# A three-layer block on one core: another order at the launch, and two weight parts split later in the second block

## The chip, the cores and the metric

The kernel runs on one core of one Trainium2 chip. The metric is the device time of one execution in microseconds (us), the median over several runs. In the rows, PE is TensorE's matmul side and PEld its weight load, DVE is VectorE, ACT ScalarE, POOL GpSimd, SP SyncE; SPq, ACTq and POOLq are DMA issues on the queues of these engines.

## The reference

One sequence of 256 tokens of width 1024 in fp32. Twice (`l` = 0, 1) a block of four mixers, cross attention and an MLP; then a second block with its own mixers and a mixture of experts. Cut to what the change touches:

```
h = rms_norm(x, ln_mix_pre[l]);  z = h @ w_in[l]        # l = 0 is the launch
s = q @ k.T * scale + bias_f[t5_bucket(t - s)]          # rel_bias, the same for both l

# second block
log_a = 8 * sigmoid(gate_r) * log_sigmoid(lam);  a = exp(log_a)
u = sqrt(-expm1(2 * log_a)) * (sigmoid(gate_i) * xr)
h = scan over time of h = a * h + u                     # the recurrence
y_c = conformer_conv(xc)                                # 31 taps, layer norm, silu, 256x256
y = concat(rms_norm(y_a), rms_norm(h * gelu(xg)), rms_norm(y_c))
x = x + y @ w_out                                       # then router and 32 experts
```

## The kernel before, in words

Each engine has a program of its own, written out by hand (`tensor`, `scalar`, `vector`, `pool`, `sync`), and nothing reorders it: an instruction behind a waiting one waits too. `P["name"]`, `A[...]`, `V[...]` are counts of what PE, ACT and DVE have finished.

**Units.** All large weights come as units of up to 1 MB through a ring of four slots, loaded by SP in order (`load`). A unit is used in two parts: ACT copies its rounded high part (`upper`, L1306, `hl<-ring`), DVE subtracts to get the low part (`lower_part`, L1953), and PE multiplies three times (`mm3`). `unit()` on ACT and DVE splits up to `LOOK` = 2 units ahead of the one that PE is about to use. SP loads a unit into a slot when the low part of the unit that had it is made. Four units of the second block, the convolution's taps, are not split (`whole`): PE reads them raw, and their slots come free only when PE is done with them:

```
if had is not None and (whole(had) or P.way == "few" and had >= n_ring):
    sp.wait_ge(s_pe, P["unit", had])
elif had is not None:
    sp.wait_ge(s_dve, V["lo", had])
```

**Launch.** ACT's queue loads constants `cst` (with the identity for transposes), parameters `par`, `x` (to `resid`) and `CO` (to `arena`: mask and one-hot rows for the bias). All engines wait for all four. PE makes `rowb`, the bias by distance; ACT copies it out; POOL writes it to memory and reads it back with every row shifted by one (`hank`, `arena<-scratch`); PE turns these rows (`C("rev")`, four matmuls `psum<-arena,cst` 128x384 called "bias"), DVE adds the mask, POOL stores the result (`bias_d<-arena`, semaphore `s_bias`). Beside it run the first norm (ACT Square and Sqrt, DVE scale by the gain `gn`), PE's transposes, and the cuts of the turned x into high and low parts (`norm_cut`, into `ht`). ACT and DVE wait for `s_bias` and only then split units 0, 1, 2; PE then runs the projections `kcks`, `q`, `kw` (units 0, 1, 2: 48, 48 and 24 matmuls) and `vg` (unit 3).

**Second block.** On PE: projections, scores (`z`) of head groups 0 to 2, `zx`, sums (`cum`) 0 and 1, `xg`, `taps(0)`, the gates `wa` and `wx`, sums 2, `weighted` 0 and 1, `taps(1)`, scores 3, `weighted` 2, `taps(2)`, sums 3, `taps(3)`, a group norm, `cmean`, `weighted` 3, `cvar` and on to the output projection `tok_out(axv, "bout")` with the four units of the output weights, here w0 to w3. w0 goes into the slot of `taps(0)`, w1 into that of `taps(1)`. The recurrence's lane on ACT and DVE: tanh of the gates, `t3` = tanh(log a), `uvar`, its root `ustd`, two scans, the gelu product, `gnsq`; head group 3 goes between (`logits`, `keeps`, `log_keep`, `log_weight`).

Of the kernel before, what the change touches and what calls it, by code (L numbers as in the profile page):

```python
# [21 lines left out]
LOOK = 2  # L22
# [240 lines left out]
def build(nc, W, CW, CS, CO, PR, PR2, GB, x_in, mem_in, out, scratch, bias_d, gate_d):  # L263
    ctx = ExitStack()
    with ctx:
# [96 lines left out]
        m0 = Place()  # L362
# [205 lines left out]
        def tensor(pe, branch):  # L568
# [3 lines left out]
            def bank(*name, keep=False):  # L572

                b, before = turn.keep(name) if keep else turn.take(name)
                if before in freed:
                    of, n = freed[before]
                    pe.wait_ge(of.sem, n)
                banks[name] = b
                return b

            def mm(o, pairs, start=True, stop=True, skip=False):
                n = len(pairs)
                for i, (a, b) in enumerate(pairs):
                    ins = pe.matmul(o, a, b, start and i == 0, stop and i == n - 1, skip)
                return ins
# [89 lines left out]
            pe.wait_ge(s_const, 16)  # L675
            pe.wait_ge(s_par, 16)
            pe.wait_ge(s_x, 16)
            pe.wait_ge(s_once, 16)
            b = bank("rowb")
            mm(psum[0:4, b, :], [(R("rel")[0:32, :], m0.onehot[0:32, :])]).then_inc(s_pe, P("rowb"))  # L680
            for l in range(2):
                L = layers[l]
                norm(L.nmix.xn, "mix", l)
                if l == 0:
                    pe.wait_ge(s_hank, 32)
                    for h in range(4):
                        b = bank("bias", h)
                        mm(psum[:, b, 0:384], [(C("rev"), m0.hank[:, h, :])]).then_inc(s_pe, P("bias", h))
# [3 lines left out]

                pe.wait_ge(s_dve, V["mix", l])
                proj(hTv, "kcks", l)
                proj(hTv, "q", l)
# [587 lines left out]
        def scalar(ac, branch):  # L1283
# [65 lines left out]
            def inverse_root(o, eps, scale, *name):  # L1349
# [4 lines left out]
                act(o, o, ACT.Exp, *name, scale=-0.5)  # L1354

            ac.dma_start(cst[:, :], CS).then_inc(s_const, 16)
            ac.dma_start(par[:, :], PR).then_inc(s_par, 16)
            ac.dma_start(Xv, x_in.rearrange("b (t p) d -> p (b t) d", t=2)).then_inc(s_x, 16)
            ac.dma_start(arena[:, 0:896], CO[:, 0:896]).then_inc(s_once, 16)
            ac.wait_ge(s_const, 16)  # L1360
            ac.wait_ge(s_par, 16)
            ac.wait_ge(s_x, 16)
            ac.wait_ge(s_once, 16)
            ac.wait_ge(s_pe, P["rowb"])
            copy(m0.rowb[0:4, :], psum[0:4, banks["rowb",], :], "rowb")
            gone("rowb")
            for l in range(2):
                L = layers[l]
                if l == 0:
                    for t in range(2):  # L1370
                        norm(Xv, L.nmix, t, "mix", l)
                    for t in range(2):
                        norm_cut(hTv, t, "mix", l)
                if l == 0:
                    ac.wait_ge(s_bias, 16)
# [370 lines left out]
            gone("xg")  # L1746
            for _ in range(4):
                unit()
            for nm, dst, o in (("wa", t1, 0), ("wx", t2, 2)):
# [12 lines left out]
            ac.wait_ge(s_dve, V["uvar"])  # L1762
            act(t1, t1, ACT.Sqrt, "ustd")
            ac.wait_ge(s_dve, V["gelu"])
            act(t3, t3, ACT.Tanh, "gelu", scale=math.sqrt(2.0 / math.pi))
            weights(3)
            ac.wait_ge(s_pe, P["cu"])
# [132 lines left out]
        def vector(ve, branch):  # L1900
# [97 lines left out]

            ve.wait_ge(s_const, 16)
            ve.wait_ge(s_par, 16)  # L2000
            ve.wait_ge(s_x, 16)
            ve.wait_ge(s_once, 16)
            for l in range(2):
                L = layers[l]
                if l == 0:
                    for t in range(2):
                        norm(Xv, L.nmix, t, "mix", l)
                    for t in range(2):
                        norm_cut(hTv, t, "mix", l)
                    for h in range(4):  # L2010
                        ve.wait_ge(s_pe, P["bias", h])
                        tt(m0.bm[:, h, :], psum[:, banks["bias", h], 0:384], m0.causal, ADD, "bias")
                        gone("bias", h)
                    ve.wait_ge(s_bias, 16)
# [463 lines left out]
            unit()  # L2478
            for _ in range(4):
                unit()  # L2480
            ve.wait_ge(s_act, A["lam"])
# [14 lines left out]
            ve.wait_ge(s_act, A["t3"])  # L2496
            ts(t1, t3, -1.0, None, ADD, None)
            rec(t1, t1)
            stt(t1, t3, 2.0, t1, MUL, MUL, "uvar")
            tt(t3, b2.xg, b2.xg, MUL)  # L2500
# [10 lines left out]
            tt(t3, b2.yc[1], b2.yc[1], MUL, "gnsq", 1)  # L2511
            log_weight(3)
            ve.wait_ge(s_act, A["ya", 2])
            tt(b2.zq[:, 0:3, :], b2.yc[0][:, 0:3, :], b2.yc[0][:, 0:3, :], MUL)
# [175 lines left out]
        def pool(gp, branch):  # L2690
# [22 lines left out]

            gp.wait_ge(s_const, 16)
            gp.wait_ge(s_par, 16)
            gp.wait_ge(s_x, 16)
            gp.wait_ge(s_once, 16)
            gain("mix0")
# [291 lines left out]
```

## Time and profile before

| | us |
|---|---|
| median of 3 runs (lowest, highest) | 2109.21 (2103.8, 2111.39) |
| the profiled execution, its own time | 2104.69 |
| its span | 2102.9 |
| PE busy in the span | 1915.1 (91%) |
| DVE busy | 1426.7 (68%) |
| ACT busy | 1168.5 (56%) |

1.79 us lie outside the span. Mean granted clock of TensorE 0.961. The page's line of 40 slices shows PE at 7 to 9 tenths everywhere but in the first slice (4), with three slices of 7 in a row at 28 to 30 (1419 to 1577 us: the end of the second block's mixers, and the router), and the DMA engines at 9 tenths and some 375 GB/s only in the experts' stage, slices 31 to 39.

### The profile page before, as it was taken

Reading aid. Unit: us, or ns where it says so; the run is one execution under the profiler, and the core shown is the slowest. Engines: PE = TensorE matmul, PEld = TensorE weight load, DVE = VectorE, ACT = ScalarE, POOL = GpSimd, SP = SyncE. Lnnn points to the kernel's source line nnn. Section 1 sums busy time; section 2 is a strip of 40 time slices with the busy share of each in tenths; the row PEclk is TensorE's granted clock in tenths of the full one; section 3 lists DMA queues with packets and bytes.
Section 4 is the critical chain, followed back from the end, with each engine's and each line's share of the span. In section 5 each row is a group of like instructions: output and inputs, shape, how many; then the busy total and the mean of one; then the engine's idle time right before and its main releaser. Section 6 shows DMA issues by size and latency. Waiting matters only on the chain.

```text
span 2102.9 us, 30304 instructions
## 1 busy us (share of the span) xinstructions
PE 1915.1 (91%) x12946; PEld 1747.3 (83%) x12946; DVE 1426.7 (68%) x1425; ACT 1168.5 (56%) x1310; POOL 76.5 (4%) x94
## 2 busy tenths in 40 slices
PE   4999997988999889997997999897779999999997
PEld 3989997987998889997997999796668888888885
DVE  3686547545555677637645555755679999999995
ACT  2644344544444554333644444454368888888884
POOL 0000013000000000013000000000000000000000
PEclk9999998998999999999998999998879999999998
DMA  7333374524554333356542555332259999999993
GB/s 265 127 141 136 119 266 162 200 101 142 193 189 159 156 141 131 127 178 243 186 159 105 190 195 181 134 121 86 94 224 374 375 375 380 377 379 374 375 391 135
DMA packets 64524, 440.87 MB, mean 210 GB/s; under 512 B 7372, under 2 KB 7372, under 8 KB 14592
## 3 DMA queue, kind: packets, MB, share of 16 engines
q1 hardware_dynamic: 55296, 399.63, 50.6%
q0 software_dynamic: 8096, 35.30, 4.5%
q10 hardware_dynamic: 992, 3.93, 0.5%
q8 instruction: 104, 1.70, 0.3%
q14 instruction: 36, 0.29, 0.0%
HBM read 428.61 MB, written 10.23 MB: 209 GB/s over the span
## 4 chain that ended last, share of the span: by engine, by line
PE 65%; DVE 22%; ACT 8%; issue 2%; POOL 1%; DMA 1%; DVEq 0%; ACTq 0%; POOLq 0%
PE psum L188 64%; DVE ring_low L202 6%; ACT hl L198 3%; DVE arena L212 3%; DVE ht L202 2%; DVE rounded L202 2%; DVE rounded L212 2%; DVE arena L202 2%; ACT arena L198 1%; PE psum L192 1%; POOL arena L202 1%; DVE hl L202 1%; ACT rounded L198 1%; DVE arena L225 1%; DVE resid L202 1%
## 5 line engine op out<-in xcount | busy, mean ns | idle before, releaser
L202 DVE TENSOR_TENSOR hl<-ring,hl 128x2048 fp32r<-128x2048 f32 (+1 forms) x190 | 433.9, 2286 | 350.7 <-ACT hl L198 350.3
L188 PE MATMUL psum<-ht,hl 128*128 128x256 f32 x4992 | 630.2, 288 | 15.4 <-DVE hl L202 9.7
L188 PEld LDWEIGHTS psum<-ht,hl 128*128 128x128 f32 x4992 | 616.2, 195 | 25.1 <-DVE hl L202 10.3
L198 ACT ACTIVATE hl<-ring 128x2048 fp32r<-128x2048 f32 (+1 forms) x286 | 536.3, 1896 | 150.7 <-PE psum L188 122.9
L188 PE MATMUL psum<-hl,ax 128*128 128x512 f32 (+1 forms) x1608 | 351.9, 355 | 6.4 <-DVE ax L202 5.0
L198 ACT ACTIVATE arena<-psum 128x512 f32<-128x512 f32 (+5 forms) x232 | 121.0, 522 | 418.5 <-PE psum L188 405.5
L188 PEld LDWEIGHTS psum<-hl,ax 128*128 128x128 f32 x1608 | 264.8, 192 | 47.3 <-DVE ax L202 5.3
L202 DVE TENSOR_TENSOR ring_low<-ring,hl 128x2048 fp32r<-128x2048 f32 x96 | 215.3, 2285 | 19.3 <-ACT hl L198 19.1
L188 PE MATMUL psum<-arena 128*128 128x128 f32 (+6 forms) x1520 | 190.8, 291 | 30.1 <-ACT arena L198 23.5
L188 PEld LDWEIGHTS psum<-arena 128*128 128x128 f32 (+2 forms) x1520 | 174.7, 179 | 41.6 <-ACT arena L198 25.2
L188 PE MATMUL psum<-hl,ht 128*128 128x256 f32 (+1 forms) x1056 | 132.2, 287 | 26.8 <-DVE ht L212 24.0
L188 PEld LDWEIGHTS psum<-hl,ht 128*128 128x128 f32 x1056 | 129.9, 196 | 29.0 <-DVE ht L212 24.4
L188 PE MATMUL psum<-rounded 128*128 128x512 f32 (+2 forms) x640 | 137.5, 346 | 8.7 <-DVE rounded L202 3.1
L188 PEld LDWEIGHTS psum<-rounded 128*128 128x128 f32 x640 | 104.0, 197 | 25.9 <-issue 7.1
L202 DVE TENSOR_TENSOR arena<-arena 128x512 f32<-128x512 f32 (+8 forms) x133 | 87.0, 654 | 46.3 <-ACT arena L198 40.2
L202 DVE TENSOR_TENSOR rounded<-arena,hl 128x2048 fp32r<-128x2048 f32 x48 | 107.7, 2286 | 0.2
L202 DVE TENSOR_TENSOR ht<-ht_raw,hl 128x2048 fp32r<-128x2048 f32 x46 | 103.2, 2285 | 5.4 <-ACT hl L198 5.4
L188 PE MATMUL psum<-hl,hx 128*128 128x512 f32 x256 | 101.4, 396 | 1.3 <-ACT rounded L198 1.3
L188 PE MATMUL psum<-hl,rounded 128*128 128x512 f32 x256 | 101.6, 397 | 0.0
L188 PE MATMUL psum<-ax,hl 128*128 128x256 f32 x768 | 94.1, 284 | 0.0
L188 PEld LDWEIGHTS psum<-ax,hl 128*128 128x128 f32 x768 | 92.7, 192 | 1.0 <-issue 1.0
L198 ACT ACTIVATE hl<-arena 128x2048 fp32r<-128x2048 f32 x48 | 89.2, 1913 | 0.0
(121 smaller groups left out, 1897.7 us busy)
## 6 DMA issues: line engine op xcount, KB each, us to landing
ring<-W SPq DMA_DIRECT2D x284, 1024.0 KB, 5.1
arena<-W SPq DMA_DIRECT2D x48, 1024.0 KB, 7.5
ht_raw<-W SPq DMA_DIRECT2D x46, 1024.0 KB, 7.8
gate_d<-arena POOLq DMA_DIRECT2D x32, 256.0 KB, 3.8
arena<-gate_d POOLq DMA_DIRECT2D x8, 1024.0 KB, 8.0
gn<-GB POOLq DMA_DIRECT2D x10, 512.0 KB, 4.1
arena<-GB POOLq DMA_DIRECT2D x6, 512.0 KB, 4.9
ring<-W SPq DMA_DIRECT2D x4, 512.0 KB, 4.5
```

The lines of the kernel that those rows point to most:

```text
L188: return Nothing() if self.e is None else self.e.matmul(o, a, b, start=start, stop=stop, skip_group_check=skip_group_check)
L192: return Nothing() if self.e is None else self.e.transpose(o, a, ident)
L198: return self.e.activation(o, a, f, bias=bias, scale=scale)
L202: return Nothing() if self.e is None else self.e.tensor_tensor(o, a, b, op)
L212: return Nothing() if self.e is None else self.e.scalar_tensor_tensor(out=o, in0=a, scalar=s, in1=b, op0=op0, op1=op1)
L225: return Nothing() if self.e is None else self.e.reciprocal(o, a)
```

## The change

At the launch, `x` is the first load of ACT's queue, ahead of the constants. ACT, DVE and POOL no longer wait for everything: ACT and DVE run both norms of x on `s_x` alone, then split unit 0, and wait for constants, parameters and `CO` behind it; ACT's copy of `rowb` stands there too; POOL's load of the gain waits for nothing. Units 1 and 2 are split behind the cuts, ahead of the wait for `s_bias`. PE runs `kcks` ahead of the turned rows ("bias"). SP's waits are as they were.

In the second block the four `unit()` calls of the taps, which split w0 and w1, move down on ACT (from behind the copy of `xg` to behind the gelu's tanh) and on DVE (from ahead of the lambda chain to behind `log_weight(3)`). And `uvar` is worked out in another way: a*a + 1 times tanh(log a), with the sign taken in the root's scale, in place of 2 t3 / (t3 - 1): a subtraction, a reciprocal and a product of 128x512 become two products.

```diff
@@ tensor @@
-            b = bank("rowb")
-            mm(psum[0:4, b, :], [(R("rel")[0:32, :], m0.onehot[0:32, :])]).then_inc(s_pe, P("rowb"))
             for l in range(2):
                 L = layers[l]
+                if l == 0:
+                    pe.wait_ge(s_par, 16)
+                    pe.wait_ge(s_once, 16)
+                    b = bank("rowb")
+                    mm(psum[0:4, b, :], [(R("rel")[0:32, :], m0.onehot[0:32, :])]).then_inc(s_pe, P("rowb"))
                 norm(L.nmix.xn, "mix", l)
                 if l == 0:
+                    pe.wait_ge(s_dve, V["mix", l])
+                    proj(hTv, "kcks", l)
                     pe.wait_ge(s_hank, 32)
@@ scalar @@
+            ac.dma_start(Xv, x_in.rearrange("b (t p) d -> p (b t) d", t=2)).then_inc(s_x, 16)
             ac.dma_start(cst[:, :], CS).then_inc(s_const, 16)
             ac.dma_start(par[:, :], PR).then_inc(s_par, 16)
-            ac.dma_start(Xv, x_in.rearrange("b (t p) d -> p (b t) d", t=2)).then_inc(s_x, 16)
...
                         norm(Xv, L.nmix, t, "mix", l)
+                    upper()
+                    ac.wait_ge(s_const, 16)
+                    ac.wait_ge(s_par, 16)
+                    ac.wait_ge(s_once, 16)
+                    ac.wait_ge(s_pe, P["rowb"])
+                    copy(m0.rowb[0:4, :], psum[0:4, banks["rowb",], :], "rowb")
+                    gone("rowb")
                     for t in range(2):
                         norm_cut(hTv, t, "mix", l)
-                if l == 0:
+                    for _ in range(LOOK):
+                        upper()
                     ac.wait_ge(s_bias, 16)
...
             gone("xg")
-            for _ in range(4):
-                unit()
             for nm, dst, o in (("wa", t1, 0), ("wx", t2, 2)):
...
-            act(t1, t1, ACT.Sqrt, "ustd")
+            act(t1, t1, ACT.Sqrt, "ustd", scale=-1.0)
             ac.wait_ge(s_dve, V["gelu"])
             act(t3, t3, ACT.Tanh, "gelu", scale=math.sqrt(2.0 / math.pi))
+            for _ in range(4):
+                unit()
             weights(3)
@@ vector @@
                         norm(Xv, L.nmix, t, "mix", l)
+                    lower_part()
+                    ve.wait_ge(s_const, 16)
+                    ve.wait_ge(s_par, 16)
+                    ve.wait_ge(s_once, 16)
                     for t in range(2):
                         norm_cut(hTv, t, "mix", l)
+                    for _ in range(LOOK):
+                        lower_part()
...
             unit()
-            for _ in range(4):
-                unit()
             ve.wait_ge(s_act, A["lam"])
...
-            ts(t1, t3, -1.0, None, ADD, None)
-            rec(t1, t1)
-            stt(t1, t3, 2.0, t1, MUL, MUL, "uvar")
+            tt(t1, aL, aL, MUL)
+            stt(t1, t1, 1.0, t3, ADD, MUL, "uvar")
...
             log_weight(3)
+            for _ in range(4):
+                unit()
             ve.wait_ge(s_act, A["ya", 2])
@@ pool @@
-            gp.wait_ge(s_const, 16)
-            gp.wait_ge(s_par, 16)
-            gp.wait_ge(s_x, 16)
-            gp.wait_ge(s_once, 16)
             gain("mix0")
```

How the instructions stand on the engines, at two places.

ACT at the program's start, before, from the first table load on (`hl<-ring` are the units 0, 1 and 2; `tensor_done` and so on are the counts of the other engines, `once_in` is `s_once`, `bias_in` is `s_bias`):

```order
L198 ACT_TABLE_LOAD [waits once_in,x_in,tensor_done,par_in]
L198 ACTIVATE arena<-psum 4x512 [waits const_in]
L199 ACTIVATE arena<-resid 128x512 x2
L198 ACT_TABLE_LOAD [waits scalar_done]
L198 ACTIVATE arena<-arena 128x1 [waits vector_done]
L199 ACTIVATE arena<-resid 128x512 x2
L198 ACTIVATE arena<-arena 128x1 [waits scalar_done,vector_done]
L198 ACTIVATE ht<-psum 128x4x128 [waits tensor_done] x4
L198 ACTIVATE hl<-ring 128x2048 [waits tensor_done,weights_in0,vector_done,bias_in]
L198 ACTIVATE hl<-ring 128x2048 [waits weights_in1]
L198 ACTIVATE hl<-ring 128x1024 [waits weights_in2]
```

The same place in the changed kernel:

```order
L199 ACT_TABLE_LOAD
L199 ACTIVATE arena<-resid 128x512 [waits x_in]
L199 ACTIVATE arena<-resid 128x512
L198 ACT_TABLE_LOAD [waits scalar_done]
L198 ACTIVATE arena<-arena 128x1 [waits vector_done]
L199 ACTIVATE arena<-resid 128x512 x2
L198 ACTIVATE arena<-arena 128x1 [waits scalar_done,vector_done]
L198 ACTIVATE hl<-ring 128x2048 [waits weights_in0]
L198 ACTIVATE arena<-psum 4x512 [waits tensor_done,once_in,scalar_done,par_in,const_in]
L198 ACTIVATE ht<-psum 128x4x128 [waits tensor_done] x4
L198 ACTIVATE hl<-ring 128x2048 [waits weights_in1]
L198 ACTIVATE hl<-ring 128x1024 [waits weights_in2]
```

The first table load now waits for nothing, the copy of `rowb` (4x512) went from ahead of the norm to behind it and unit 0, and no unit stands behind `bias_in` any more.

DVE in the second block, the difference of the two kernels from the lambda chain to the squares of the attention's groups (`hl<-ring` x2 are w0 and w1, the `arena<-arena,psum` x2 with the next row are `log_weight(3)`):

```order
-L208 TENSOR_SCALAR arena<-arena 128x512
-L225 RECIPROCAL arena<-arena 128x512
+L202 TENSOR_TENSOR arena<-arena 128x512
 L212 SCALAR_TENSOR_TENSOR arena<-arena 128x512
 L202 TENSOR_TENSOR arena<-arena 128x512
```

```order
 L202 TENSOR_TENSOR arena<-arena,psum 128x384 x2
 L208 TENSOR_SCALAR arena<-arena 128x768
+L202 TENSOR_TENSOR hl<-ring,hl 128x2048 x2
 L202 TENSOR_TENSOR arena<-arena 128x768
 L212 SCALAR_TENSOR_TENSOR arena<-psum,arena 128x512
```

The two low parts left the place ahead of the lambda chain and stand between `log_weight(3)` and the squares that precede the product of `cmean` (the last row); in `uvar` the reciprocal is gone.

## Rows read from the trace of the kernel before

**Rows 1.** Stretch: length, busy us of PE, PEld, DVE, ACT, POOL, clock, DMA, GB/s.

```profile
1600.00:1650.00 50.00, 48.75 (x253) 40.30 (x251) 47.84 (x35) 43.90 (x38) 0.00 (x0) 1.00 0.96 378
```

**Rows 2.** DMA of 0 to 40 us: one GB/s figure per us, and issues to landing.

```profile
GB/s 0 115 107 369 410 427 459 351 418 422 409 412 126 74 442 426 389 422 412 403 21 0 69 290 373 82 324 168 4 0 0 0 233 418 135 0 80 319 432 438
cst<-CS ACTq DMA_DIRECT2D x1, 1027.0 KB, 7.9
bias_d<-arena POOLq DMA_DIRECT2D x1, 768.0 KB, 3.5
arena<-CO ACTq DMA_DIRECT2D x1, 448.0 KB, 10.8
```

**Rows 3.** Timeline of the launch: start, us, instructions merged, [idle before <-releaser].

```profile
13.10 1.86 PE L188 MATMUL psum<-arena,par 32*4 32x512 f32 x2 [13.10 <-DMA arena<-CO]
16.36 0.59 ACT L198 ACTIVATE arena<-psum 4x512 f32<-4x512 f32 x1
16.85 0.61 ACT L199 ACTIVATE arena<-resid 128x512 f32<-128x512 f32 x1
...
18.25 1.28 ACT L198 ACT_TABLE_LOAD   x1
...
22.41 0.29 ACT L198 ACTIVATE arena<-arena 128x1 f32<-128x1 f32 x1 [1.36 <-DVE arena L209]
...
23.75 1.97 PE L192 MATMUL psum<-cst,arena 128*128 128x128 f32 x8 [0.27 <-DVE arena L212]
...
25.86 4.31 PE L188 MATMUL psum<-arena,cst 128*128 128x384 f32 x7
...
34.96 4.66 ACT L198 ACTIVATE hl<-ring 128x2048 fp32r<-128x2048 f32 x3 [8.61 <-DMA bias_d<-arena]
...
37.87 5.56 DVE L202 TENSOR_TENSOR hl<-ring,hl 128x2048 fp32r<-128x2048 f32 x3
40.24 15.90 PE L188 MATMUL psum<-ht,hl 128*128 128x256 f32 x120 [9.75 <-DVE hl L202]
47.53 0.80 ACT L198 ACTIVATE arena<-psum 128x256 f32<-128x256 f32 x2 [7.91 <-PE psum L188]
...
55.98 5.48 PE L188 MATMUL psum<-hl,ht 128*128 128x140 f32 x48
```

**Rows 4.** Stretches, same columns: PE's restart at 40.2 us, and 1443 to 1453 us.

```profile
40.20:43.20 3.00, 2.96 (x14) 2.99 (x15) 3.00 (x2) 0.00 (x0) 0.00 (x0) 0.51 0.91 336
1443.00:1453.00 10.00, 5.88 (x22) 4.72 (x23) 8.85 (x21) 5.44 (x9) 0.00 (x0) 0.51 0.01 2
```

**Rows 5.** Timeline of the second block, PE.

```profile
1428.11 7.18 PE L188 MATMUL psum<-arena,ring 128*128 128x256 f32 x32
1443.04 1.65 PE L188 MATMUL psum<-arena 128*128 128x256 f32 x4 [7.10 <-ACT arena L198]
1448.77 2.00 PE L188 MATMUL psum<-arena 128*64 128x128 f32 x12 [4.08 <-ACT arena L198]
...
1460.88 6.21 PE L188 MATMUL psum<-arena,ring 128*128 128x256 f32 x28
```

**Rows 6.** The same stretch, ACT.

```profile
1440.00 1.91 ACT L198 ACTIVATE hl<-ring 128x2048 fp32r<-128x2048 f32 x1 [10.16 <-DMA ring<-W]
...
1451.35 1.72 ACT L198 ACTIVATE arena<-arena 128x768 f32<-128x768 f32 x2 [0.39 <-DVE arena L212]
...
1457.17 0.63 ACT L198 ACTIVATE arena<-arena 128x512 f32<-128x512 f32 x1
```

**Rows 7.** The same stretch, DVE.

```profile
1451.89 3.35 DVE L225 RECIPROCAL arena<-arena 128x512 f32<-128x512 f32 x1
...
1458.00 1.76 DVE L212 SCALAR_TENSOR_TENSOR arena<-arena 128x768 f32<-128x768 f32 x2
...
1465.41 0.96 DVE L202 TENSOR_TENSOR arena<-arena 128x768 f32<-128x768 f32 x1
1469.40 0.69 DVE L212 SCALAR_TENSOR_TENSOR arena<-psum,arena 128x512 f32<-128x512 f32 x1 [3.03 <-PE psum L188]
```

More of the change, by code:

```diff
@@ L675, in tensor @@
             pe.wait_ge(s_const, 16)
-            pe.wait_ge(s_par, 16)
-            pe.wait_ge(s_x, 16)
-            pe.wait_ge(s_once, 16)
-            b = bank("rowb")
-            mm(psum[0:4, b, :], [(R("rel")[0:32, :], m0.onehot[0:32, :])]).then_inc(s_pe, P("rowb"))
             for l in range(2):
                 L = layers[l]
+                if l == 0:
[3 more added lines that the diff above has]
+                    mm(psum[0:4, b, :], [(R("rel")[0:32, :], m0.onehot[0:32, :])]).then_inc(s_pe, P("rowb"))
                 norm(L.nmix.xn, "mix", l)
                 if l == 0:
+                    pe.wait_ge(s_dve, V["mix", l])
+                    proj(hTv, "kcks", l)
                     pe.wait_ge(s_hank, 32)
@@ L690, in tensor @@
                 fill = filler(l)
-                pe.wait_ge(s_dve, V["mix", l])
-                proj(hTv, "kcks", l)
+                if l:
+                    pe.wait_ge(s_dve, V["mix", l])
+                    proj(hTv, "kcks", l)
                 proj(hTv, "q", l)
@@ L1354, in inverse_root @@
                 act(o, o, ACT.Exp, *name, scale=-0.5)
+            ac.dma_start(Xv, x_in.rearrange("b (t p) d -> p (b t) d", t=2)).then_inc(s_x, 16)
             ac.dma_start(cst[:, :], CS).then_inc(s_const, 16)
             ac.dma_start(par[:, :], PR).then_inc(s_par, 16)
-            ac.dma_start(Xv, x_in.rearrange("b (t p) d -> p (b t) d", t=2)).then_inc(s_x, 16)
             ac.dma_start(arena[:, 0:896], CO[:, 0:896]).then_inc(s_once, 16)
-            ac.wait_ge(s_const, 16)
-            ac.wait_ge(s_par, 16)
             ac.wait_ge(s_x, 16)
[L1363 to L1366, printed above, removed]
             for l in range(2):
@@ L1997, in wide @@
                 return ap.broadcast_to([128, ap.shape[1], n])
-            ve.wait_ge(s_const, 16)
-            ve.wait_ge(s_par, 16)
             ve.wait_ge(s_x, 16)
-            ve.wait_ge(s_once, 16)
             for l in range(2):
```

## The prediction

> **What bounds the kernel now.** I read the stages first, by stretches. In the experts' stage nothing of this change takes part: in 50 us PE is busy 48.75 and DVE 47.84, the granted clock is 1.00 and DMA runs at 378 GB/s [rows 1]. It will come as it is, earlier or later. So the question is only when PE gets its work in the two edited places, and there I read the timeline and the chain of waits.
>
> *Launch.* The first matmul starts at 13.10, released by the load of `CO` [rows 3]. DMA runs at some 410 GB/s from 4 to 11 us [rows 2], so the early loads are bound by bandwidth and not by their issue. Then one lane runs: `rowb` on PE, ACT's copy at 16.36, two small transfers by POOL, the turned rows on PE at 25.86, masks, `bias_d`, and at 34.96 ACT, released by it, begins unit 0 [rows 3]. PE's row at 40.24 says idle for 9.75 us before, waiting for DVE's low part. x, unit 0 and the turned x were all there long before 34.96: the projections wait for splits that stand behind a semaphore they don't need.
>
> *Second block.* PE finishes `taps(1)` at 1435.3 [rows 5]. Half of scores 3 follows, and then PE stands 7.10 us for ACT. ACT's row at 1440.00 tells why: it waited 10.16 us for a DMA, which is w1 [rows 6]. w1's slot is free only when `taps(1)` is done. Behind this wait stand the tanh of the gates, which give PE the bank for the other half. Then come 4.08 us more for `weighted` 2. The granted clock from 1443 to 1453 is 0.51, the low level (1.2 GHz), after this idling [rows 4].
>
> **The change, launch.** Its loads: `cst`, first in the queue, took 7.9 us [rows 2], so x in its place (1024 KB against 1027) lands at 0.74 + 7.9 = 8.6. The gain, 512 KB, now goes at once too: 1.3 us at 410 GB/s. I take x at 9.3 (8.6 to 9.9) and `CO` 1.3 later than now, at 14.3.
>
> By x: from the first Square at 16.85 to the second root's end at 22.70 are 5.85 us, of which some 0.7 were a wait for the gain, gone now; ACT's first table load waits for nothing and is hidden. So 9.3 + 5.2 = 14.5, unit 0's high part 1.9 (a share of 4.66 for three), low part 2.2 (of 5.56 for three [rows 3]), four cuts of 0.69 (a 128x512 DVE operation, [rows 7]): 21.4. By `CO`: 14.4, `rowb` 1.9, sixteen transposes in two lots of 1.97 [rows 3], one cut on ACT and DVE, 1.3: 21.5. The two paths are equal; I take 21.5 for `kcks` against 40.24.
>
> `kcks` ran 7.25 us (40.24 until ACT's copy at 47.53, where 72 matmuls then took 8.65), because PE restarts at the low level: 0.51 in its first 3 us [rows 3, 4]. It will again: PE stands 1.5 us before, and the rates of the first 30 us are low-level ones though the record has no mark there (the turned rows take 4.31 for 7 records of 384 columns, 1.6 ns a column; taps at a clock of 1.00 take 0.87 [rows 3, 5]). `kcks` ends at 28.8.
>
> The bias lane: ACT reaches the copy of `rowb` at 16.4, PE has it at 16.3; it began at 16.36 before. So the turned rows land as before, at 25.9, and 3 us of `kcks` cover them. That is the slack for SP's loads: units 4 and 5 now follow the low parts at 18.7 and 24, beside POOL's two transfers, and 1 MB is 2.5 us of bandwidth. From the first turned matmul to `s_bias` it was 34.96 - 25.86 = 9.1. PE is warm now, which takes 2.2 off (8 records of 384 columns at 0.87 in place of 1.6): 6.9, so `s_bias` comes at 35.7, later than now by 0.7.
>
> Who waits for `s_bias`: ACT and DVE, for unit 3 only, since 0 to 2 are split. DVE's memsets took it from 34.96 to 37.9, then the low part of unit 3, 1120 columns, 1.3 at the pace of [rows 3]: 40.0. PE: 28.8 + 2.7 of turned rows + 8.65 for `q` and `kw` = 40.2. Again equal. `vg` starts at 40.3 against 55.98, **15.7 us** earlier, and from there on everything stands in its old order. If `s_bias` is late beyond 0.2 us each us counts in full; if x or `CO` is late, too. Ends: 11 (x 1.5 late, and 3 for transfers beside each other), 17.5 (x at 8.6 and `kcks` warm after its first 1.5 us).
>
> By the Trainium skill ("ScalarE: Activation LUTs", What ACT_TABLE_LOAD costs) a switch is a load of about 1.28 us and a drain of about 1.38. The row at 18.25 shows 1.28, and the span of 5.85 contains all that followed, so no drain is added here. By the page's figure the path by x would be 1.4 longer and this term 14.3.
>
> **The change, second block.** The wait for w1 leaves ACT's way. The gates' banks are free at about 1427, so PE goes through 1435.94 (1443.04 less 7.10) without a stop. From 1443.04 to the end of `taps(3)` at 1467.1 are 24.05 us; without 4.08 of waiting, and with the 5.9 us of matmuls in the slow stretch [rows 4] at twice the clock (2.9 less), 17.1 remain: `taps(3)` ends at 1453.0, **14.1** earlier.
>
> Can DVE's lane follow? Scores 3 are in by 1437.7 (1435.94 + 0.8 of matmul + 0.9). From `keeps(3)` at 1451.35 to the end of `ustd` at 1457.80 it was 6.45 [rows 6]: 1444.2. Removed on DVE are the reciprocal, 3.35, and a subtraction of 0.4, added is a product of 0.7 [rows 7]: with it DVE's own work ends at 1441.1, hidden behind ACT's `keeps(3)`; with the old form it would end at 1444.2 and delay `log_keep(3)` by about 2.5. From the scaled input of the scan (1459.0) to the squares (1465.41) are 6.4: 1450.6. Here the two low parts come in, 2 x 2.3 = 4.6: 1455.2, squares 0.96: 1456.2, and the product of `cmean` starts then, against 1469.40: **13.1** earlier. PE has `cmean` ready at 1455.3, so the moved low parts cost 0.9 of the 14.1. ACT's share of w0 and w1 (3.8) lies from 1446.4 to 1450.2, before the weights of group 3 are asked for at 1450.6: hidden, with 0.4 to spare. w1's load landed at 1440: covered. Behind that stand the same instructions; w2 and w3 load behind `taps(2)` and `taps(3)`, 14 earlier. Ends: 9 (the lane pays all 4.6) and 14.2 (PE's own).
>
> **Sum.** 15.7 + 13.1 = 28.8 off the profiled execution's 2104.69: 2075.9; off the median 2109.21: 2080.4. The profiled run lies near the lowest of the three; I say 2078. Ends: 20 to 31.7 off, 2073 to 2089.
>
> **Rivals.** (a) The bias lane sets the launch. `hank` and `bias_d` now share the DMA engines with units 4 to 6. For: bandwidth is full at 410 GB/s when several loads run; `CO`, 448 KB behind others, took 10.8, `bias_d` 3.5 [rows 2]. If both of POOL's late transfers take 10.8, that is 7.3 on `bias_d` and 3 or more past the slack on the rows: the launch gives 5, the sum 18: 2089. Against: from 22 to 35 us the figures of [rows 2] lie mostly below 330 and often at 0. Chance 0.12.
> (b) The second block gives half. The chain there is carried by DVE, whose unit parts were free in the wait, and some step that I count as hidden isn't: 6.5 in place of 13.1, 2085. For: DVE's slack in my sum is negative already. Chance 0.12.
> (c) No change: PE's work between the edited places is re-timed, and later waits (POOL's gate transfers, loads) take back over 20 us, 2100. Against: nothing in the program is tied to the time since its start. 0.04.
> (d) Slower: a busier PE is granted less. If the clock in the experts' stage, about 540 us long with PE busy 97%, fell below 1.00, each hundredth would cost 5 us; from 0.05 on it eats the gain, from 0.08 on the time ends above 2115. Against: the clock was 1.00 there at PE's densest [rows 1]. 0.02.
> My forecast, both terms within their ends: 0.70.
>
> **The numbers.** Forecast, (a) and (b) lie between 2066 (lowest run 2103.8, both upper ends, some noise) and 2092; I give 2066 to 2094. Such a kernel is told from no change at about 0.5%, 10.5 us: faster is below 2098.7. Faster 0.70 + 0.12 + 0.12 = 0.94; same 0.04; slower 0.02.
>
> **What the profile will show.** Right: the first Square near 9.5 us; `kcks` near 21.5; turned rows behind it near 29; `vg` near 40.3 with no PE idle between `kcks` and `vg` above 1 us. In the second block no PE gap between `taps(0)` and `taps(3)`, clock 1.00, the two low parts on DVE right behind `log_weight(3)`, and about 13 us less from `xg` to `cmean`'s product. Wrong: PE idle ahead of `q` or `vg` waiting for `bias_d` or DVE (a); PE idle ahead of sums 3 or more than 1 us ahead of `cvar` (b).

## The result, and the profile after

The changed kernel takes 2084.89 us, median of 4 runs (2082.65 to 2085.21), against 2108.58 of 4 runs of the kernel before (2103.8 to 2111.39): a ratio of 0.9888, with an interval of 0.9868 to 0.9907. It is faster. The forecast was 2078 with a range of 2066 to 2094. The profiled execution took 2085.21, its span is 19.6 shorter than that of before, and 28.8 had been forecast.

The page, its first and third line:

```profile
span 2083.3 us, 30300 instructions
...
PE 1918.9 (92%) x12946; PEld 1752.3 (84%) x12946; DVE 1423.3 (68%) x1424; ACT 1167.9 (56%) x1310; POOL 76.5 (4%) x94
```

PE is busy 3.8 us longer than before with the same work, while the span is shorter: a first sign that it ran more of it at a lower clock.

The launch, timeline of all engines (start, duration, then as in [rows 3]):

```profile
10.17 0.63 ACT L199 ACTIVATE arena<-resid 128x512 f32<-128x512 f32 x1 [6.07 <-DMA resid<-x]
...
11.59 1.28 ACT L198 ACT_TABLE_LOAD   x1
12.88 0.29 ACT L198 ACTIVATE arena<-arena 128x1 f32<-128x1 f32 x1
...
14.90 1.86 PE L188 MATMUL psum<-arena,par 32*4 32x512 f32 x2 [14.90 <-DMA arena<-CO]
...
22.07 6.02 PE L188 MATMUL psum<-ht,hl 128*128 128x256 f32 x48 [1.71 <-DVE ht L202]
27.92 2.74 PE L188 MATMUL psum<-arena,cst 128*128 128x384 f32 x8
...
31.61 0.54 POOL L231 DMA_DIRECT2D bias_d<-arena  x1 [9.08 <-DVE arena L202]
...
36.71 0.80 ACT L198 ACTIVATE arena<-psum 128x256 f32<-128x256 f32 x2 [12.96 <-DMA bias_d<-arena]
...
39.61 1.26 DVE L202 TENSOR_TENSOR hl<-ring,hl 128x1120 fp32r<-128x1120 f32 x1
...
40.93 10.14 PE L188 MATMUL psum<-hl,ht 128*128 128x140 f32 x48 [1.64 <-DVE hl L202]
50.99 8.53 PE L188 MATMUL psum<-arena 128*47 128x64 f32 x80
```

The order is the one that the change wrote: the first Square waits for x alone and starts at 10.17, `kcks` at 22.07, then the turned rows at 27.92, then `q` and `kw`, done by 39.3. `bias_d` is issued at 31.61 and lands when ACT goes on, at 36.71; DVE's memsets and the low part of unit 3 follow, and PE, which has stood (done nothing, waiting) for 1.64 us, begins `vg` at 40.93. Before it was 55.98 [rows 3]: 15.05 earlier. But `vg` now takes 10.14 where it took 5.48, and the 80 records behind it take 8.53. The windows show why (columns: stretch, its length, busy time of each engine with its records, granted clock, DMA's busy share, GB/s):

```profile
38.00:41.00 3.00, 1.36 (x12) 1.16 (x11) 2.61 (x5) 1.67 (x4) 0.03 (x1) 1.00 0.86 322
41.00:43.00 2.00, 2.00 (x12) 2.00 (x12) 1.90 (x4) 1.97 (x2) 0.00 (x0) 0.59 1.01 406
...
49.00:51.00 2.00, 2.00 (x11) 1.87 (x10) 0.00 (x0) 0.00 (x0) 0.00 (x0) 0.50 1.02 418
...
55.00:57.00 2.00, 2.00 (x32) 1.92 (x31) 0.00 (x0) 0.22 (x2) 0.00 (x0) 0.99 0.00 0
```

Ahead of the stand the clock is 1.00. Behind it it is 0.50, TensorE's lower level of 1.2 GHz, from 41.4 to 55.1 us, and PE is busy all the time (2.00 of 2.00 in each row).

The second block. PE's rows from `taps(1)` on, then DVE's:

```profile
1421.07 7.18 PE L188 MATMUL psum<-arena,ring 128*128 128x256 f32 x32
...
1430.57 7.18 PE L188 MATMUL psum<-arena,ring 128*128 128x256 f32 x32
...
...
1450.66 4.54 PE L188 MATMUL psum<-arena,cst 128*128 128x256 f32 x12 [1.75 <-DVE arena L202]
```

```profile
1434.89 0.96 DVE L212 SCALAR_TENSOR_TENSOR arena<-arena 128x768 f32<-128x768 f32 x1 [0.59 <-ACT arena L198]
...
1437.37 0.69 DVE L212 SCALAR_TENSOR_TENSOR arena<-arena 128x512 f32<-128x512 f32 x1 [1.52 <-ACT arena L198]
...
1443.60 4.49 DVE L202 TENSOR_TENSOR hl<-ring,hl 128x2048 fp32r<-128x2048 f32 x2
1448.12 0.96 DVE L202 TENSOR_TENSOR arena<-arena 128x768 f32<-128x768 f32 x1
1449.19 0.69 DVE L212 SCALAR_TENSOR_TENSOR arena<-psum,arena 128x512 f32<-128x512 f32 x1
```

The waits of 7.10 and 4.08 of [rows 5] are gone. The two moved low parts (1443.60, 4.49 for two) stand ahead of the squares (1448.12) and of `cmean`'s product (1449.19). From the start of `taps(0)` to this product are now 40.35 us and were 53.52, 13.17 less; to the start of the output projection it is only 11.90 less.

Some landmarks serve for this and all experiments, each the start of a row in one engine's timeline: `kcks` and `vg` on PE; "scores", the first scale of a score tile on DVE behind `vg`; `taps(0)`; `cmean`'s product; `bout`, the output projection's first matmul. With the old launch PE stands ahead of `kcks` and not ahead of `vg`, and one experiment moves the stand ahead of `kw`: their cells are empty.

| us | kcks | PE stands ahead of vg | vg | scores | taps(0) | cmean's product | bout | span |
|---|---|---|---|---|---|---|---|---|
| before | 40.24 | | 55.98 | 65.91 | 1415.88 | 1469.40 | 1491.59 | 2102.9 |
| after | 22.07 | 1.64 | 40.93 | 57.38 | 1408.84 | 1449.19 | 1472.65 | 2083.3 |

The 19.6 us, from landmark to landmark: 8.53 up to the scores (15.05 at `vg`, 6.52 of it lost by then); 1.49 lost from there to `taps(0)`; 11.90 from there to `bout`; 0.66 behind it.

### The profile page after: what moved, and what is told of

Read it like the earlier page. It is cut to its first block, busy times and chain, and to the rows that moved or that the text cites. A ratio compares the mean times of both kernels' runs of the same rounds, so it can differ in the third digit from the quotient of the medians.

```text
span 2083.3 us, 30300 instructions
## 1 busy us (share of the span) xinstructions
PE 1918.9 (92%) x12946; PEld 1752.3 (84%) x12946; DVE 1423.3 (68%) x1424; ACT 1167.9 (56%) x1310; POOL 76.5 (4%) x94
## 4 chain that ended last, share of the span: by engine, by line
PE 65%; DVE 22%; ACT 8%; issue 2%; POOL 1%; DMA 1%; DVEq 0%; ACTq 0%; POOLq 0%
PE psum L188 64%; DVE ring_low L202 6%; ACT hl L198 3%; DVE arena L212 3%; DVE ht L202 2%; DVE rounded L202 2%; DVE rounded L212 2%; DVE arena L202 2%; ACT arena L198 2%; PE psum L192 1%; DVE hl L202 1%; POOL arena L202 1%; ACT rounded L198 1%; ACT gn L198 1%; ACT L198 1%
## 5 line engine op out<-in xcount | busy, mean ns | idle before, releaser
L188 PEld LDWEIGHTS psum<-arena 128*128 128x128 f32 (+2 forms) x1520 | 175.2, 180 | 28.8 <-ACT arena L198 13.9
L188 PE MATMUL psum<-hl,ht 128*128 128x256 f32 (+1 forms) x1056 | 136.7, 293 | 28.5 <-DVE ht L212 24.0
L188 PEld LDWEIGHTS psum<-hl,ht 128*128 128x128 f32 x1056 | 134.2, 202 | 30.8 <-DVE ht L212 24.4
L202 DVE TENSOR_TENSOR arena<-arena 128x512 f32<-128x512 f32 (+10 forms) x134 | 87.7, 655 | 47.0 <-ACT arena L198 40.8
```

Of the source, the lines that this page charges most:

```text
L188: return Nothing() if self.e is None else self.e.matmul(o, a, b, start=start, stop=stop, skip_group_check=skip_group_check)
L202: return Nothing() if self.e is None else self.e.tensor_tensor(o, a, b, op)
```

## The experiments

My theory: a stand of PE of 1.6 us ahead of `vg` makes the clock fall, and this costs some 6.5 us, four times the stand. The second block gives about what was forecast. The rival: the low stretch comes from something else (the DMA traffic, or the clock's own course), and the stand is beside the point.

### One half of the change each

The launch alone (the second block as before), and the second block alone (the launch as before).

> The changed launch with the second block as before. Theory: the launch's term stands alone. vg starts at 40.9 us, the clock falls there as in the changed kernel, the first scale of the scores on DVE comes near 57.4, 8.5 us earlier than before, and the second block has its 7.1 us of PE idle again. Time 8 to 9 us below the kernel before, less what low stretches of the clock take later: 2100 (2098 to 2102). Rival: the two parts need each other, or the launch's 8.5 us are lost before the second block; then the time is within 3 us of the kernel before.

> The changed second block with the launch as before. Theory: about 12 us less (13.2 until the product of cmean, 1.3 given back behind it by a lower clock): 2096.5 (2094 to 2099). From the start of taps(0) to the product of cmean it takes 40.3 us in place of 53.5. Rival: part of the 12 us belongs to the launch, and this kernel gains under 8.

### The stand taken away, and a stand made elsewhere

Unit 3 is split ahead of the wait for `s_bias`, so that `vg` waits for nothing behind it:

```diff
-                    for _ in range(LOOK):
+                    for _ in range(LOOK + 1):
                         upper()
                     ac.wait_ge(s_bias, 16)
...
                         tt(m0.bm[:, h, :], psum[:, banks["bias", h], 0:384], m0.causal, ADD, "bias")
+                    lower_part()
```

> The changed kernel with unit 3 split ahead of the wait for s_bias too (ACT behind unit 2, DVE behind the four mask additions), so that PE doesn't stand before vg. Theory: the clock fell at 41.5 us because PE stood 1.64 us ahead of vg; without that gap it stays at 1.00, vg takes 5.5 us and not 10.1, and the first scale of the scores comes near 49.3 in place of 57.4. Time 8 us below the changed kernel, 2077. Rival: the clock falls there for another reason (what PE runs in vg, or the time since the start); then only the 1.6 us are gained, the scores come near 55.7, and the time is 2083.

And as after, but PE waits for the low part of unit 3 already ahead of `kw`, so that the stand comes 24 matmuls earlier and longer:

```diff
                 proj(hTv, "q", l)
+                if l == 0:
+                    pe.wait_ge(s_dve, V["lo", 3])
                 proj(hTv, "kw", l)
```

> The changed kernel with one wait of PE moved: it waits for the low part of unit 3 ahead of kw, not ahead of vg, so that it stands some 4.6 us there and restarts with kw's 24 matmuls of 256 columns. Theory: after the restart the clock is low for about 3 us, as at 40.2 us in the kernel before; then vg runs at 1.00 in 5.5 us and the scores' first scale comes near 55.5, some 2 us earlier than in the changed kernel though PE stood longer. Rival: the low stretch is about 13.6 us long whatever follows the gap; kw takes 5.8, vg 10.1, and the scale comes near 63, the time 6 us above the changed kernel.

What was measured, these four against 2110.8 of the kernel before on the same chip:

| | time (range), us | ratio (interval) | kcks | stand | vg | scores | taps(0) | cmean's product | bout | span |
|---|---|---|---|---|---|---|---|---|---|---|
| launch only | 2094.85 (2092.57 to 2097.8) | 0.9934 (0.9911 to 0.9958) | 22.02 | 0.22 | 41.10 | 51.13 | 1405.33 | 1459.06 | 1481.59 | 2092.4 |
| block 2 only | 2096.43 (2091.5 to 2097.19) | 0.9933 (0.9909 to 0.9957) | 38.81 | | 54.94 | 64.87 | 1420.60 | 1460.95 | 1484.06 | 2094.8 |
| unit 3 early | 2080.30 (2077.81 to 2083.82) | 0.9859 (0.9836 to 0.9883) | 21.94 | 0 | 39.04 | 49.40 | 1408.13 | 1448.49 | 1471.60 | 2082.0 |
| stand ahead of kw | 2085.11 (2082.81 to 2089.61) | 0.9888 (0.9862 to 0.9913) | 21.88 | | 47.06 | 57.38 | 1410.37 | 1450.71 | 1473.45 | 2084.4 |

PE's timeline of unit 3 early, and of the stand ahead of `kw`, with two of the latter's windows ahead of it and behind:

```profile
39.04 5.48 PE L188 MATMUL psum<-hl,ht 128*128 128x140 f32 x48
44.91 6.63 PE L188 MATMUL psum<-arena 128*47 128x64 f32 x80 [0.39 <-ACT arena L198]
```

```profile
41.77 5.49 PE L188 MATMUL psum<-ht,hl 128*128 128x256 f32 x24 [5.54 <-DVE hl L202]
47.06 5.87 PE L188 MATMUL psum<-hl,ht 128*128 128x140 f32 x48
```

```profile
38.00:41.00 3.00, 0.00 (x0) 0.00 (x0) 2.65 (x4) 1.75 (x3) 0.86 (x2) 1.00 0.58 195
...
43.00:48.00 5.00, 5.00 (x26) 5.00 (x25) 3.67 (x4) 1.87 (x3) 0.00 (x0) 0.51 0.52 198
```

With the stand gone, `vg` takes 5.48 as in [rows 3], and the scores begin at 49.40, 8 us before the changed kernel's and 16.5 before those of before. With the stand ahead of `kw` the clock is 0.51 behind it and `kw` at that pace: in the launch the fall came with the stand, at either place, and didn't come without it. Whether any stand of this length is followed by one is another question, and the last section answers it with no. The low stretch was 6.8 us long, not 13.7, so the scores came at 57.38, between the theory's 55.5 and the rival's 63: it has no fixed length. The median with unit 3 early is 4.6 below the changed kernel's and not 8, and the intervals of the two ratios overlap; the landmarks carry this reading.

The launch alone has the same launch as the changed kernel, and I expected the fall there again and 2100 us. Yet PE stood for 0.22 only, the clock stayed, the scores came 14.8 earlier than before, and the time is 2094.85. What differs is `bias_d`, which landed 5.1 us after its issue in the changed kernel's profile and here after

```profile
bias_d<-arena POOLq DMA_DIRECT2D x1, 768.0 KB, 3.7
```

`kcks` ran 7.66 us here and not 6.02, but that moves PE and the bias lane alike, since the turned rows stand behind it. From the first turned row on PE has 11.4 us of work up to `vg`; the lane needs 3.7 to the issue of `bias_d`, its transfer, and 4.2 more. So the stand is the transfer's time less some 3.5, and this holds in all seven profiles, here and below, in which `vg` waits for this lane: 5.1, 5.0, 4.7, 4.1, 3.9, 3.7 and 3.5 us of transfer go with stands of 1.64, 1.61, 1.24, 0.66, 0.42, 0.22 and 0. With unit 3 early `bias_d` took 6.0, and PE didn't stand, since `vg` no longer waits for it.

The halves give 15.95 and 14.37 off the median, 30.3 together, near the 28.8 of the forecast, where both in one kernel gave 24 to 25. The low clock behind the stand (6.5, and 4.9 in the second execution below) is about as large as this difference, but only profiled executions show where the clock was low, so that it explains the medians isn't shown. Within the second block they add up, too: `taps(0)` to `cmean`'s product is 53.73 in the old form and 40.35 in the new, whatever the launch.

### Again, and three small edits

The changed kernel once more; the changed kernel with the old `uvar`; w0's parts (three of the four `unit()` calls) earlier, on ACT behind "t3" and on DVE ahead of `logits(3)`, with w1's left where they are; and this with unit 3 early, both together.

> The changed kernel again, for a second profile. Theory: which idle gaps of PE make its clock fall, and for how long, differs from one execution to the next of the same instructions, so the launch's low stretch (41.4 to 55.1 us in the first profile) can be absent here, and low stretches elsewhere differ by some 3 to 20 us in sum between 60 us and the second block. The stretch from taps(0) to the output projection stays at 63.8 us within 0.6. Rival: the low stretches belong to the instructions, and come again at the same places with the same lengths.

> The changed kernel with uvar in the old form (subtraction, reciprocal, product), the low parts staying behind log_weight(3). Theory: DVE's own work ahead of log_keep(3) grows by 3.1 us from 1434.3, so log_keep(3) ends at 1438.4 in place of 1435.9, sums 3 start 0.8 later and the scaled input of the scan 1.0 later: from the start of taps(0) to the product of cmean 41.4 us in place of 40.35, time 1 us up. Rival 1: the old form was hidden, 40.35. Rival 2: it counts in full, 43.4.

w0's parts early, on DVE (ACT likewise):

```diff
+            for _ in range(3):
+                unit()
             logits(3)
...
             log_weight(3)
-            for _ in range(4):
-                unit()
+            unit()
```

> The changed kernel with w0 split where both engines stand idle for scores 3 (ACT behind t3, DVE ahead of logits(3)), and only w1 behind log_weight(3). Theory: the two low parts cost the lane 1.4 us against PE's own pace (cmean ready at 1447.8, its product on DVE at 1449.2), so with one of them the product starts when PE is ready, 39.1 us behind the start of taps(0), and the time falls by 1.2 us or a little more. Rival: w0's load lands after 1424 or its split holds up logits(3); then scores 3 are read later, PE gets a gap ahead of sums 3, and the time rises by up to 2 us.

> The changed kernel with unit 3 split ahead of s_bias and w0 split early. Theory: the gains add, 4.6 (as measured for unit 3 alone, of 8 us gained locally) and 1.2: 2079 against 2085 for the changed kernel. Rival: the clock's low stretches further on take the launch's part back wholly, and the time is above 2082.

Measured against 2109.24 of the kernel before:

| | time (range), us | ratio (interval) | stand | vg | scores | taps(0) | cmean's product | bout | span |
|---|---|---|---|---|---|---|---|---|---|
| after, again | 2084.09 (2081.78 to 2088.07) | 0.9877 (0.9862 to 0.9892) | 1.61 | 42.33 | 57.18 | 1412.86 | 1453.19 | 1475.97 | 2086.3 |
| old uvar | 2077.85 (2075.22 to 2087.76) | 0.9857 (0.9836 to 0.9877) | 0.66 | 41.31 | 51.34 | 1405.58 | 1447.15 | 1470.26 | 2075.9 |
| w0 early | 2082.14 (2075.80 to 2090.93) | 0.9876 (0.9854 to 0.9899) | 1.24 | 40.40 | 50.43 | 1403.15 | 1442.18 | 1465.16 | 2076.4 |
| both | 2078.37 (2076.51 to 2079.57) | 0.9855 (0.9837 to 0.9873) | 0 | 40.65 | 50.57 | 1403.67 | 1442.69 | 1465.70 | 2075.4 |

The second execution of the changed kernel shows the stand and the fall again, where I had thought that they could be absent. PE's timeline and the windows:

```profile
42.33 9.48 PE L188 MATMUL psum<-hl,ht 128*128 128x140 f32 x48 [1.61 <-DVE hl L202]
```

```profile
42.30:45.00 2.70, 2.67 (x18) 2.67 (x18) 2.47 (x5) 2.55 (x4) 0.00 (x0) 0.72 0.98 410
45.00:53.00 8.00, 8.00 (x44) 7.87 (x44) 4.58 (x3) 3.13 (x4) 0.00 (x0) 0.50 0.70 260
```

The old `uvar`, DVE's timeline:

```profile
1434.28 1.75 DVE L212 SCALAR_TENSOR_TENSOR arena<-arena 128x768 f32<-128x768 f32 x2
```

From `taps(0)`, `log_keep(3)` starts at 28.70 in place of 26.05, 2.65 later; of it 1.52 were a wait of DVE for the root anyway (the row at 1437.37 above), and `cmean`'s product is 1.22 later (41.57 against 40.35), as I expected. But this kernel's median is 6 us lower than the changed kernel's, where I expected 1 us more. Its profile says where: it lost nothing behind `vg`, and the stretch from `bout` to the end took 605.6 where it is 609.7 to 611.3 in all others. Nor is it the chance of one profile: five of its six executions (2075.2 to 2078.5) lie below every execution of the changed kernel, at a mean granted clock of 0.966 to 0.968, against 0.959 to 0.964 there. Why it is granted more stays open. Its lane is slower by 1.2 and its time is lower: no total of these settles an edit of one microsecond, and the landmarks do.

With w0's parts early, DVE and then PE:

```profile
1420.15 2.29 DVE L202 TENSOR_TENSOR hl<-ring,hl 128x2048 fp32r<-128x2048 f32 x1 [3.47 <-ACT hl L198]
...
1442.18 0.69 DVE L212 SCALAR_TENSOR_TENSOR arena<-psum,arena 128x512 f32<-128x512 f32 x1 [0.99 <-PE psum L188]
```

```profile
1443.65 2.87 PE L188 MATMUL psum<-arena,cst 128*128 128x256 f32 x12 [0.43 <-DVE arena L202]
```

The median is not to be told from the changed kernel's, the landmarks are. One low part now lies in DVE's wait for the gates; DVE waits 0.99 us for PE's `cmean` and not the other way round. The distance is 39.03, 1.32 less. PE's wait ahead of `cvar` is 0.43 in place of 1.75, and `cvar` with the norm takes 2.87 in place of 4.54; it takes 2.87, too, in three profiles in which PE waited 1.74 and the clock didn't fall. The two edits together have these 1.3 us and the early scores (50.57), and no execution above 2079.57, where the changed kernel in the same comparison has none below 2081.78. The old `uvar`'s median is 0.5 lower still, with one execution at 2087.76.

### The gain's load, and the loads beside the bias

POOL's load of the gain waits for x (`gp.wait_ge(s_x, 16)` ahead of `gain("mix0")`), which tells what it costs x:

> The changed kernel with POOL's load of the gain issued only when x has landed. Theory: the 512 KB of the gain, moved beside x, are what delayed x from 8.6 to 10.15 us; without them x lands near 8.8 and CO near 13.5 in place of 14.87. The gain then lands near 8.8 + 7 = 16, 2.5 us after DVE needs it, so the norms end later and kcks starts near 23 to 24 in place of 22.0: a loss of 1 to 2 us there. Rival: x's own form (256 rows of 4 KB) makes it slower than cst, and it lands near 10 again.

SP holds back units 5 and 6 until the bias is stored, which tells what they cost `bias_d`:

```diff
+                if u == 5:
+                    sp.wait_ge(s_bias, 16)
```

> The changed kernel with SP waiting for s_bias ahead of its load of unit 5. Theory: bias_d took 5.08 us and not 3.5 because units 5 and 6 load beside it (about 390 GB/s at 31 to 34 us); without them it takes 3.5, s_bias comes near 35.1, PE's stand ahead of vg falls from 1.6 us to below 0.3 and the clock doesn't fall there; scores' first scale near 50 to 51. Rival: bias_d takes 5 us anyway, or units 5 and 6 now come late (needed at 43.7 us on ACT) and PE stands further on.

And the kernel before once more, for the spread of its stretches.

> The kernel before again, for a second profile. Theory: the product of cmean comes 53.5 to 53.8 us behind the start of taps(0) and the scores' first scale at 65 to 66 us, as in the first profile, while the time from the one to the other stage (1350.0 us in the first) differs by up to 9 us with the low stretches of the clock. Rival: these 1350 us are the same within 1 us, and the longer ones of the changed kernels (1351 to 1359) are a cost of the change.

Against 2110.41 of the kernel before:

| | time (range), us | ratio (interval) | kcks | stand | vg | scores | taps(0) | cmean's product | bout | span |
|---|---|---|---|---|---|---|---|---|---|---|
| gain behind x | 2084.22 (2080.46 to 2084.8) | 0.9873 (0.9858 to 0.9888) | 22.87 | 0.42 | 42.07 | 52.10 | 1407.86 | 1448.20 | 1471.67 | 2082.4 |
| units behind bias | 2088.33 (2082.19 to 2092.97) | 0.9891 (0.9871 to 0.9911) | 22.03 | 0 | 40.82 | 55.63 | 1412.70 | 1453.04 | 1475.83 | 2086.5 |
| before, again | 2110.37, one run | | 38.55 | | 54.54 | 64.47 | 1421.57 | 1475.13 | 1497.32 | 2108.6 |

The loads of the launch, DMA issues (KB each, us to landing), of the changed kernel, of the gain behind x, and of the units behind the bias:

```profile
resid<-x ACTq DMA_DIRECT2D x1, 1024.0 KB, 9.4
...
bias_d<-arena POOLq DMA_DIRECT2D x1, 768.0 KB, 5.1
...
arena<-CO ACTq DMA_DIRECT2D x1, 448.0 KB, 12.5
```

```profile
resid<-x ACTq DMA_DIRECT2D x1, 1024.0 KB, 7.8
...
arena<-CO ACTq DMA_DIRECT2D x1, 448.0 KB, 10.8
```

```profile
arena<-CW POOLq DMA_DIRECT2D x1, 1024.0 KB, 12.1
...
bias_d<-arena POOLq DMA_DIRECT2D x1, 768.0 KB, 3.5
```

PE's timeline with the units held back, and a window of it behind the stand:

```profile
40.82 5.58 PE L188 MATMUL psum<-hl,ht 128*128 128x140 f32 x48
49.54 8.23 PE L188 MATMUL psum<-arena 128*47 128x64 f32 x80 [3.14 <-issue]
```

```profile
50.15:53.55 3.40, 3.40 (x36) 3.40 (x34) 0.00 (x0) 0.00 (x0) 0.00 (x0) 0.50 1.04 429
```

The gain beside it costs x 1.6 us (9.4 against 7.8) and `CO` 1.7; but `kcks` starts 0.8 later without it beside x, since DVE then waits for the gain. Units 5 and 6 cost `bias_d` 1.6 in the changed kernel's profile (5.1 against 3.5 here and in [rows 2]), and with them held back PE has no stand ahead of `vg`. Beside the same two units it took anything from 3.7 to 6.1 in nine profiles; why it differs wasn't found. They are only moved: `CW`, which took 6.5, now takes 12.1 beside them. PE waits for it (`s_cmp`) right behind `vg`: issued at 37.38, it lands at 49.5, and PE goes on at 49.54 after a stand of 3.14 us, for which the profile names no releaser. Here the clock falls, and the scores come at 55.63 where I expected 50 to 51.

## Why the prediction was right, and where it was off

**Loads and norms.** x came at 10.17 and not 9.3: the gain's load costs it 1.6, and I had counted 0.7. From x to the end of the second root it took 5.3 (forecast 5.2). `CO` came at 14.9 for 14.3, and `kcks` started at 22.07 for 21.5: right but for the load. The Trainium skill's drain ("ScalarE: Activation LUTs", What ACT_TABLE_LOAD costs) is not seen here either: the load at 11.59 takes 1.28 and the next activation starts 0.01 behind it.

**PE's part of the launch.** `kcks` was forecast at 7.25; it ran 6.02 here, 6.0 in three other profiles of this launch and 7.5 to 7.7 in six. Turned rows, `q` and `kw` were done at 39.3 (forecast 40.2).

**The bias lane.** Forecast 6.9 from the turned rows to `s_bias`, measured 8.8: 1.6 of the difference is `bias_d` beside units 5 and 6, as the run that holds them back shows. So `s_bias` came at 36.7 for 35.7, and `vg` at 40.93 for 40.3. That this is off by 0.65 only is in part luck: the lane began at 27.9 and not at 28.8, because `kcks` was fast. In the second execution of the same kernel `kcks` ran 7.50 and `vg` starts at 42.33, 2.0 after the forecast. Rival (a) was right in kind, since the lane is what `vg` waits for; the lateness cost 0.65, and not the 11 of its price.

**The step that failed** is "from there on everything stands in its old order". The order was the old one, the pace wasn't. I had called PE's path and the lane "again equal" and priced a late lane at its lateness, "each us counts in full". The lane was 1.64 behind PE, and PE's stand was followed by a low clock: `vg` and the 80 records behind it cost 6.5 more. With the stand removed, the scores came 16.5 earlier (forecast 15.7 for `vg`); with it, 8.5. I had charged `kcks` for a restart at the low level, and `vg`, behind a stand of its own, for none. In the markers I had named an idle above 1 us as what would make me wrong, but gave it no price beyond its length.

**Second block.** No wait from `taps(0)` to `taps(3)`; the lane to `cmean`'s product 13.17 shorter for 13.1, and 40.33 to 40.36 long in all six other profiles of this form. The old `uvar` would delay `log_keep(3)` by 2.5: it does by 2.65. The moved low parts cost 0.9: they cost 1.3 (w0 early). Mis-sized is "Behind that stand the same instructions", which was priced at nothing: 1.27 are given back up to `bout`. PE stands 1.75 ahead of `cvar` in place of 0.43, and the clock falls there, but this is not where they go: from `cvar`'s start to the eight matmuls behind it are 9.02 us, and were 8.90, since PE waits less afterwards (4.48 for 6.04). 0.8 of them lie behind the start of the last four matmuls ahead of `bout`, which take 2.07 at a clock of 0.50 and took 1.13 at 1.00. In five other profiles of the new form 0.5 to 0.9 are given back, and 1.3 in one.

**The sum.** 28.8 forecast, 19.6 measured in the span: 0.65 for the late `vg`, 6.5 for the clock behind it, 1.3 behind `cmean`; the remaining 0.8 is 1.5 lost between scores and `taps(0)` less 0.7 regained at the end. That stretch runs the same instructions in every kernel here, and it differs as much between two executions of one kernel, so I give it no cause. Rival (b)'s marker, PE idle ahead of `cvar`, is seen at a fifth of its price of 6.6; of (c) and (d) nothing is: from `bout` to the end, the experts' stage in it, it takes 610.65 for 611.31.

## What to carry to other kernels

Where a sum makes two paths to TensorE "equal", price the case that the other one is late by a microsecond or two with the clock behind it: here 1.6 us of standing were followed by 6.5 us more in matmuls in one profile of the changed kernel and by 4.9 in the other, and splitting unit 3 ahead of a wait that it doesn't need removed both. But a stand of one length isn't followed by a low clock each time (last section), so take it as a risk and not as a fixed price. When a load or a unit is moved out of one critical wait, look at which transfer it then stands beside; holding units back from `bias_d` moved the stand to the next load, and it was longer there. Judge an edit of one or two microseconds by the distance between two landmarks that enclose it, and not by the total.

## What was not expected of the hardware

**The same instructions at another clock.** Between the scores and `taps(0)` lie about 9500 matmul records that no edit touches. Window rows of this stretch, of before, of before again, of after, and of unit 3 early:

```profile
65.91:1415.88 1349.97, 1258.38 (x9503) 1197.32 (x9501) 812.79 (x910) 624.97 (x795) 72.22 (x83) 0.97 0.45 161
```

```profile
64.47:1421.57 1357.10, 1265.58 (x9503) 1204.44 (x9502) 812.77 (x910) 624.82 (x795) 72.06 (x83) 0.96 0.45 160
```

```profile
57.38:1408.84 1351.46, 1259.60 (x9502) 1198.19 (x9501) 812.85 (x910) 624.74 (x795) 72.22 (x83) 0.97 0.45 161
```

```profile
49.40:1408.13 1358.73, 1267.03 (x9502) 1205.52 (x9501) 812.82 (x910) 624.95 (x795) 72.06 (x83) 0.96 0.45 161
```

It takes 1349.97 and 1357.10 us in two executions of the kernel before, and 1351.46 and 1358.73 here, with PE's busy time up and down by the same amounts and DVE's and ACT's equal within 0.3: the clock's low stretches are longer in some executions. That is 7 us, a third of what the change gives, and it hides the 8 us that unit 3 early won in the launch from its own profile (its span is 1.3 shorter than the changed kernel's); its median is 4.6 lower. What decides it stays open: no run varied it on purpose.

**How long a low stretch lasts.** With PE busy all the time, it was 13.7 us in the changed kernel, 10.2 in its second execution, and 6.8 behind the stand of 5.54 ahead of `kw`. The clock stayed at 1.00 behind stands of 0.22, 0.42, 0.66 and 1.24 us, in kernels that have the same launch but for one load; it fell behind those of 1.61 and 1.64.

**A stand's length doesn't decide.** Elsewhere in the same profiles the clock stays behind longer stands. In all 13 PE stands 1.64 or 1.65 us some 9 us ahead of `taps(0)`, and the clock stays at 1.00. Ahead of `cvar` it falls behind 1.75 or 1.90 in five profiles and stays behind 1.74 in three. And PE once stands 3.1 us up to a place between 82 and 99 us: in nine profiles the clock falls with it, for 3.4 or 6.8 us, in four it doesn't. The kernel before has both; its first and second execution, rows of PE's timeline, then windows:

```profile
98.90 4.74 PE L188 MATMUL psum<-arena 128*64 128x128 f32 x64 [3.12 <-ACT arena L198]
97.44 7.61 PE L188 MATMUL psum<-arena 128*64 128x128 f32 x64 [3.12 <-ACT arena L198]
```

```profile
98.90:103.00 4.10, 4.10 (x60) 4.10 (x61) 0.42 (x1) 0.38 (x1) 0.00 (x0) 1.00 0.88 360
97.44:103.00 5.56, 5.55 (x44) 5.56 (x46) 0.12 (x1) 0.38 (x1) 0.00 (x0) 0.50 0.64 270
```

The same 64 matmuls behind the same stand take 4.74 us in one execution and 7.61 in the other. So the same stand is followed by a fall in one execution and not in another. Why it comes in one execution and not in the next, and why the low stretches differ in length, wasn't found.
